# A decoder layer on one core: another order of the first splits and of the attention's steps, heads in alternating halves of the PSUM banks, and the residual rows loaded at two other points

## What is computed

```python
proj = x @ w_in                      # c_b, c_c, c_h, q, k, v, o (1024 wide each), 8 gate columns
y_conv = c_b * causal_dwconv(c_c * c_h, w_sc_conv)
h = mlstm(q, k, v, i_pre, f_pre)     # 4 heads of 256: decay-weighted causal scores, times v, normalised
h = sigmoid(o) * head_layer_norm(h)
x = layer_norm(alpha * x + concat(y_conv, h) @ w_out)
hid = causal_dwconv(x @ w_up) + b;  val, gate = split(hid)
out = layer_norm(alpha * x + (silu(gate) * val) @ w_down)
```

## Time and profile before

| | |
|---|---|
| time, median of 3 runs | 2162.56 us (2161.64 to 2162.69) |
| the profiled execution's own time | 2164.61 us |
| its span, first to last instruction | 2162.8 us |
| PE busy with matmuls | 2081.5 us (96%) |
| DVE / ACT / POOL busy | 1787.0 / 1055.2 / 328.5 us |
| mean granted TensorE clock | 0.986 of full speed |

### The profile page before, as it was taken

One profiled execution on the slowest core, in us unless ns is written; L12 is line 12 of the kernel. 1 busy time (PEld: TensorE's weight loads), 2 busy tenths in 40 slices (PEclk: granted clock), 3 DMA queues, 4 the chain that ended last, 5 costly groups with the idle time before them and its releaser, 6 DMA issues. The chain is left out here.

```text
span 2162.8 us, 28480 instructions
## 1 busy us (share of the span) xinstructions
PE 2081.5 (96%) x10903; PEld 1782.9 (82%) x10903; DVE 1787.0 (83%) x2188; ACT 1055.2 (49%) x1310; POOL 328.5 (15%) x305
## 2 busy tenths in 40 slices
PE   9899999998998998999999999999999999999995
PEld 7788888886876887888888888888888878888874
DVE  7687777776437997988888888888888789999998
ACT  5344444444324446555555555555555455444442
POOL 2011101100001304011111111111011023221220
PEclk9999999999999999999999999999999999999998
DMA  6788877752238625898888887887778888775463
GB/s 221 213 214 207 204 193 189 182 162 101 78 122 258 181 70 158 224 246 235 218 210 211 238 222 198 214 235 211 192 196 218 268 233 224 205 244 145 137 194 78
DMA packets 115815, 419.02 MB, mean 194 GB/s; under 512 B 10988, under 2 KB 25356, under 8 KB 109408
## 3 DMA queue, kind: packets, MB, share of 16 engines
q1 hardware_dynamic: 75648, 270.56, 35.5%
q0 software_dynamic: 40032, 146.64, 35.1%
HBM read 353.72 MB, written 31.46 MB: 178 GB/s over the span
## 5 line engine op out<-in xcount | busy, mean ns | idle before, releaser
L2346 PE MATMUL ps<-xb,slot_hi 128*128 128x512 f32 x2408 | 605.7, 393 | 9.1 <-DVE hid L1831 9.0
L2346 PEld LDWEIGHTS ps<-xb,slot_hi 128*128 128x128 f32 x2408 | 433.9, 189 | 89.1 <-issue 9.5
L2350 PEld LDWEIGHTS ps<-xb,slot_lo 128*128 128x128 f32 x2400 | 328.2, 191 | 23.6
L2350 PE MATMUL ps<-xb,slot_lo 128*128 128x256 f32 x2400 | 335.4, 283 | 0.0
L2210 PE MATMUL ps<-xm,m_slot_hi 128*128 128x512 f32 x1120 | 282.3, 394 | 8.7 <-DVE m_hid L1495 8.7
L2210 PEld LDWEIGHTS ps<-xm,m_slot_hi 128*128 128x128 f32 x1120 | 202.5, 190 | 45.6 <-issue 9.2
L1800 DVE TENSOR_TENSOR slot_lo<-unit_odd,slot_hi 128x1024 fp32r<-128x1024 f32 x153 | 187.1, 1223 | 34.5 <-ACT slot_hi L1168 34.5
L1168 ACT ACTIVATE slot_hi<-unit_odd 128x1024 fp32r<-128x1024 f32 x154 | 162.8, 1058 | 106.9 <-PE ps L2350 75.6
L1800 DVE TENSOR_TENSOR slot_lo<-unit_even,slot_hi 128x1024 fp32r<-128x1024 f32 x147 | 179.7, 1222 | 36.0 <-ACT slot_hi L1168 35.7
L1168 ACT ACTIVATE slot_hi<-unit_even 128x1024 fp32r<-128x1024 f32 x147 | 155.5, 1058 | 94.3 <-PE ps L2350 75.6
L2386 PE MATMUL ps<-slot_hi,hc 128*128 128x512 f32 x744 | 184.8, 390 | 4.7 <-DVE acc L1997 4.7
(11 more groups left out here) (257 smaller groups left out, 3414.1 us busy)
## 6 DMA issues: line engine op xcount, KB each, us to landing
unit_odd<-w_up SPq DMA_DIRECT2D x88, 512.0 KB, 6.2
unit_even<-w_up SPq DMA_DIRECT2D x84, 512.0 KB, 6.5
da<-w_down SPq DMA_DIRECT2D x16, 2048.0 KB, 11.9
unit_odd<-w_up POOLq DMA_DIRECT2D x44, 512.0 KB, 8.5
unit_even<-w_up POOLq DMA_DIRECT2D x42, 512.0 KB, 8.5
m_unit_odd<-w_feat SPq DMA_DIRECT2D x40, 512.0 KB, 4.4
m_unit_even<-w_feat SPq DMA_DIRECT2D x40, 512.0 KB, 4.5
da<-w_down POOLq DMA_DIRECT2D x20, 1024.0 KB, 10.5
```

The costliest lines, as they stand in the source:

```text
L2346: pe.matmul(ps[:, up_bank(m, i), :], hi[:, P * j:P * j + P], xb[:, i, j, :, :].rearrange("p r t -> p (r t)"), start=fresh and j == 0, stop ...
L2350: last = pe.matmul(ps[:, up_bank(m, i), 256:512], lo[:, P * j:P * j + P], xb[:, i, j, 0, :], start=False, stop=j == 7, skip_group_check=no ...
```

## The change

- The first tiles: ACT and DVE split tile 5 straight after tile 4 and put the sums of x between the later splits; the subtraction for P7 goes from POOL to DVE (`sum_raw(3)`). Two `raw` buffers swap places, so that block A21 of the mix weights (which S1 needs) is loaded after the split of tile 6 and A12 after that of tile 7, the other way round than before. ACT splits the second mix product's weights before it copies v out of the banks.
- The gates' arithmetic starts one product later and its first block is cut into four steps, one for each of n = 4..7; all later gate steps come four products later.
- `spread_g(0)` no longer waits for the last mix sums; its bank is 1 in place of 2 (`scores(0)` now has the wait).
- Banks: q8..q15 accumulate in banks 0 to 3; heads 0 and 1 have scores in banks 2 and 3, heads 2 and 3 in 6 and 7; the values of heads 0, 1 and 3 are in banks 0 to 3, those of head 2 in 4 to 7. Which waits this moves is seen in the diff.
- Steps of the heads after other tiles (`SPREAD`, `SCORE`, `VALUE`); on ACT and DVE the reading of the last v and o tiles comes ahead of the other steps of its tile.
- `x_rows` h = 1 is loaded when head 3's norm is done, h = 0 where both were loaded.

```diff
-SPREAD = {STAGE0 - 1: 0, STAGE0 + 3: 1, STAGE0 + 7: 2, STAGE0 + 11: 3}
-SCORE = {STAGE0 + 1: 0, STAGE0 + 4: 1, STAGE0 + 8: 2, STAGE0 + 12: 3}
-VALUE = {STAGE0 + 2: 0, STAGE0 + 6: 1, STAGE0 + 10: 2, STAGE0 + 14: 3}
+SPREAD = {STAGE0 - 1: 0, STAGE0 + 3: 1, STAGE0 + 8: 2, STAGE0 + 12: 3}
+SCORE = {STAGE0 + 1: 0, STAGE0 + 5: 1, STAGE0 + 10: 2, STAGE0 + 14: 3}
+VALUE = {STAGE0 + 2: 0, STAGE0 + 6: 1, STAGE0 + 11: 2, STAGE0 + 16: 3}
+SCORE_BANK, VALUE_BANK = (2, 2, 6, 6), (0, 0, 4, 0)
...
+        def row_bank(r):
+            return 0 if V1_LAST < r <= O_LAST[0] else 4
...
-            for b, r in ((A12, 6), (A21, 7), (A22, 8)):
+            for b, r in ((A21, 6), (A12, 7), (A22, 8)):
...
-            pool.wait_ge(t_raw, 1)
-            pool.tensor_tensor(t_raw_of["P7"], x_quarter(1, 1), x_quarter(0, 1), ALU.subtract).then_inc(t3_raw, 1)
             mix_s1(1)
...
+                if c == 0:
+                    pool.wait_ge(norm_step, 13 * HEADS)
+                    pool.wait_ge(p_l, HEADS)
+                    pool.wait_ge(g_spread, HEADS)
+                    load_rows(1)
                 for p in (0, 2):
                     out_s1(c, p)
                 if c == 0:
                     pool.wait_ge(y_turned, 8)
-                    for h in (1, 0):
-                        pool.dma_start(rows[:, 2 * h:2 * h + 2, :], x_rows[2 * h:2 * h + 2].rearrange("c p n -> p c n")
-                                       ).then_inc(res_in[h], 16)
+                    load_rows(0)
...
             split(4)
+            split(5)
             sum_raw(0)
             sum_raw(1)
-            split(5)
+            split(6)
             sum_raw(2)
             sum_lo(0)
-            split(6)
+            sum_raw(3)
+            split(7)
             sum_lo(1)
             sum_lo(2)
-            split(7)
             sum_lo(3)
...
-                if n == 3:
-                    gates_a()
-                if n == 5:
+                if 4 <= n < 8:
+                    gates_a(n - 4)
+                if n == 9:
                     gates_b()
...
-                        if first and kk == 0 and r == STAGE0 and c < 2:
-                            if c == 0:
+                        if first and kk == 0 and c == 0:
+                            if r == STAGE0:
                                 pe.wait_ge(hid_dve, N_READS * (N_UNITS - 1) + READS["P3"])
-                        elif first and kk == 0 and r == V1_LAST + 1:
-                            pe.wait_ge(vp_lo, NS + c + 1)
-                        elif first and kk == 0 and r == O_LAST[0] + 1:
-                            pe.wait_ge(o_sig, c + 1)
-                        last = mm3(ps[:, B_ROWS + c, :], x_block(k, c, later),
+                            elif r == V1_LAST + 1:
+                                pe.wait_ge(head_read, 2 * NS)
+                            elif r == O_LAST[0] + 1:
+                                pe.wait_ge(head_read, 3 * NS)
+                                pe.wait_ge(p_raw, HEADS * NS)
+                        last = mm3(ps[:, row_bank(r) + c, :], x_block(k, c, later),
...
-                    pe.wait_ge(hid_dve, N_READS * N_UNITS)
                 else:
                     pe.wait_ge(head_read, NS * h)
+                    if h == 2:
+                        pe.wait_ge(vp_lo, 2 * NS)
-                pe.matmul(ps[:, B_S, :], head_rows[:, h, :], g_row[:, :], start=True, stop=True).then_inc(g_spread, 1)
+                pe.matmul(ps[:, SCORE_BANK[h] - 1, :], head_rows[:, h, :], g_row[:, :], start=True, stop=True).then_inc(g_spread, 1)
...
+                if h == HEADS - 1:
+                    pe.wait_ge(o_sig, NS)
```

More of the change, by code:

```diff
@@ L158, in build @@
         eps = at("eps", [P, 2], SM + 3424)
-        raw = [at(f"raw{i}", [P, 1024], WR + a * KB) for i, a in enumerate((28, 32, 20, 24))]
+        raw = [at(f"raw{i}", [P, 1024], WR + a * KB) for i, a in enumerate((28, 32, 24, 20))]
         w_hi = [at(f"w_hi{i}", [P, 1024], WR + (36 + 4 * i) * KB, F32R) for i in range(SPLIT)]
@@ L724, in out_s1, with load_rows @@
                                accum_op=ALU.add, max_dma_last_dim=4096).then_inc(s1_added[p // 2], 16)
+            def load_rows(h):
+                pool.dma_start(rows[:, 2 * h:2 * h + 2, :], x_rows[2 * h:2 * h + 2].rearrange("c p n -> p c n")
+                               ).then_inc(res_in[h], 16)
             def out_s3(c, p):
@@ L902, in sum_split @@
                 what = SUMS[i]
[L903 to L906, removed]
+                act.wait_ge(t_raw, i + 1)
                 act.activation(xm[:, SLOT[what], :, 0, :], t_raw_of[what], ACT.Copy,
@@ L1039, in _ @@
             split(9)
+            mix_split(1)
             act.wait_ge(tile_done, GATES)
             for c in range(NS):
-                act.activation(v_stage[:, c, :], ps[:, B_ROWS + c, :], ACT.Copy).then_inc(v_got, 1)
-            mix_split(1)
+                act.activation(v_stage[:, c, :], ps[:, 4 + c, :], ACT.Copy).then_inc(v_got, 1)
             act.wait_ge(consts_in, 16 * 7)
@@ L1082, in rows_work @@
             def rows_work(r):
+                if r == V1_LAST:
+                    act.wait_ge(tile_done, r + 1)
+                    act.wait_ge(pv_done, 2 * NS)
+                    for c in range(NS):
+                        act.activation(v_hi[:, c, :, 0:HD], ps[:, row_bank(r) + c, :].rearrange("p (h e) -> p h e", h=2),
+                                       ACT.Copy).then_inc(vp_hi, 1)
+                if r in O_LAST:
+                    act.wait_ge(tile_done, r + 1)
+                    if r == O_LAST[0]:
+                        act.wait_ge(scores_done, NS * HEADS)
+                    else:
+                        act.wait_ge(y_ready, NS)
+                    for c in range(NS):
+                        act.activation(sig[:, c, :], ps[:, row_bank(r) + c, :], ACT.Sigmoid).then_inc(o_sig, 1)
                 if r in SPREAD:
@@ L1096, in rows_work @@
                     act.activation(std[:, :], mv[:, :, 1], ACT.Sqrt, bias=eps[:, 0:1]).then_inc(head_std, 1)
[L1097 to L1110, removed]
             split(STAGE0 + 2)
@@ L1628, in rows_work_b @@
             def rows_work_b(r):
+                if r == V1_LAST:
+                    for c in range(NS):
+                        dve.wait_ge(vp_hi, NS + c + 1)
+                        dve.tensor_tensor(v_lo[:, c, :, 0:HD], ps[:, row_bank(r) + c, :].rearrange("p (h e) -> p h e", h=2),
+                                          v_hi[:, c, :, 0:HD].bitcast(F32), ALU.subtract).then_inc(vp_lo, 1)
                 if r in SPREAD:
@@ L1643, in rows_work_b @@
                     norm_heads(VALUE[r])
-                if r == V1_LAST:
-                    for c in range(NS):
-                        dve.wait_ge(vp_hi, NS + c + 1)
-                        dve.tensor_tensor(v_lo[:, c, :, 0:HD], ps[:, B_ROWS + c, :].rearrange("p (h e) -> p h e", h=2),
-                                          v_hi[:, c, :, 0:HD].bitcast(F32), ALU.subtract).then_inc(vp_lo, 1)
                 if r in O_LAST:
@@ L2149, in scores @@
                         at = P * j
-                        last = mm3(ps[:, B_S + j % 2, 0:SC_W[j]],
+                        last = mm3(ps[:, SCORE_BANK[h] + j % 2, 0:SC_W[j]],
                                    (qk_hi[:, 2 + d, at:at + P], qk_lo[:, 2 + d, at:at + P]),
@@ L2226, in _ @@
                 mix_product(n)
[L2227 removed]
+                if n == 33:
                     turn_gates()
```

83 lines of the change are left out of this document (43 added, 40 removed).

## The result

The changed kernel takes 2126.6 us, median of 4 runs (2125.0 to 2134.2); the kernel before, on the same chip, 2162.2 us (4 runs). The ratio is 0.984, 95% interval 0.982 to 0.987: 1.6% faster. The forecast was 2123.0 us in a range of 2118 to 2131. The profiled execution, the fastest of the four, took 2125.04 us with a span of 2123.3, the very numbers that the prediction gives for it.

The account below looks back on a forecast made before the run. The prediction took PE's time as the bound, with 43.5 us of stops and slow stretches in reach; less 2.0, 0.9, 0.8 and 0.3 us this gave 39.5 us, so 2123.0 us, range 2118 to 2131.

Parts of the forecast that it names:

- The base: PE's time within reach: 33.0 us of stops, 1.8 of overlaps and 8.7 of slow stretches, 43.5 in all.
- First tiles: Tiles 5 and 6: w_lo stops of 1.7 us go; POOL's subtraction on DVE, 1.2 to 2.5 us, is covered.
- The 0.82 us at tile 1: PE's wait in front of tile 1, ahead of everything the change moves; expected to stay.
- A21 ahead of A12: Start of mix stage: A21's earlier load moves the S1, S2, S3 chain about 5.4 us earlier, removing P7's 3.1 us stop.
- The gates and the mix turns: Mix stage: gates in four steps remove P3's 5.6 us stop; longer DVE turns cost 0.8 us, bounds 0 to 3.2.
- spread_g(0): Before q0: the 1.1 us stop for bank 2 goes, and with it the slow q0, 1.75 us.
- scores(0): Third score block's wait for a bank that DVE reads: the stop grows to 2.0 us, bounds 0.7 to 3.7.
- half slow tile: Lower clock after the stop in scores(0): between 0 and 1.75 us, half taken, 0.9.
- Margins: spread_g(2) and values(3): v_lo's margin near half a us, values(3) just covered; each miss 0 to 2 us, taken as 0.
- Rows of x: Residual sums: the 8.4 us stop for load h = 1 goes; h = 0 may be late, 0 to 5.2 us, taken as 0.3.
- the rival of 2130 us: Residual rows: load h = 0 becomes the stop, up to 5.2 us, and the slow part of 2.1 stays; chance 0.14.
- The clock rival: Tiles q1 to q23 held at the lower clock: slower than before, 2177 us with ten such tiles; chance 0.02.

Follow-up runs that it names:

- e2_heads: The kernel before with only the heads' part: step tables, banks of heads, v and o tiles, and their waits; 2145.6 us, ratio 0.992.
- e3_rows: The kernel before with only the residual rows' loads at their new places; 2155.9 us, ratio 0.996.
- e10_pool_sum: The changed kernel with P7's sum of x back on POOL, the splits staying ahead of the sums; 2127.4 us, ratio 0.983.
- e8_a12_first: The changed kernel with A12 loaded ahead of A21 again and the two raw buffers in their old order; 2127.4 us, ratio 0.984.
- e12_again: The changed kernel measured once more with no edit; 2129.7 us, ratio 0.985.
- e5_s2_load: The changed kernel with A21 going out first, ahead of A11, among the second unit's weight loads; 2124.1 us, ratio 0.982.
- e11_old_banks: The changed kernel with v and o tiles back in banks 4 to 7 and heads in 0 to 3, steps at their new tiles; 2136.8 us, ratio 0.987.
- e1_first: The kernel before with only the first part: splits ahead of sums, P7's sum on DVE, A21 first, gates in steps; 2154.0 us, ratio 0.996.

## Why the prediction was right

**The base held.** That stops are worth their idle time plus 0.16 us plus their slow stretch is borne out where nothing else mixes in: from spread_g(1) to the transposes of y the prediction has 16.4 us and 16.4 were won, in the whole change and in e2_heads; the residual rows have 10.4, and 10.4 were won, in the whole change and in e3_rows alone.

**First tiles.** Both w_lo stops are gone: 2.0 forecast, 1.9 measured. P7's sum takes 2.28 us on DVE, within the 1.2 to 2.5 given, and its cover held (e10_pool_sum: no matter where it is done). The 0.82 us at tile 1, which the prediction let stand, are not in this profile; they come and go with the execution (0.79 in e8_a12_first, none in e12_again), so the sum has luck in it here as well.

**A21 ahead of A12.** The effect was right (P7's 3.1 us gone), but the cause given isn't needed: e8_a12_first has A12 first and no stop at P7. The new splits had moved the whole chain.

**The gates and the mix turns** are the step that failed. The prediction put 0.8 us (0 to 3.2) on the excess of DVE's turns, as work. It came to 4.0 us, outside the bounds. The work is as forecast, 0.8 us (e5_s2_load). The rest the prediction did not have: 1.5 us of wait, S2's for a DMA of the next unit, with PE's next sums queued behind it, and 1.6 us of the lower clock after the stop. That unit's loads go out when the mix stage starts (58.80 us, 60.73 before), so they don't get earlier with what PE gains inside the stage. The prediction asked what stood behind a wait for each wait that the change adds; this one was in the code before, at no cost because PE was late.

**spread_g(0)** and the slow q0: gone as forecast, 11.6 - 8.6 = 3.0 us by q1.

**scores(0)**: forecast 2.0 and 0.9 for its clock. The stop is 1.25 us, inside the bounds, and the clock cost nothing: from it to spread_g(1) PE takes 16.1 us in all nine profiles that have it, and the granted clock is 1.00 (468.8 to 486.5 us after the change). The Trainium skill's section that the prediction set against its half slow tile ("TensorE: Matmul & The Clock Gate", "HAM oscillation — how this bites in real kernels") was right here. P4 differs from it: a stop of 2.19 us there was followed by a stretch at the lower clock that cost 1.6 us, and the measurement decides.

**Margins.** v_lo was the narrow one: DVE's four splits end at 519.68 + 2.48 = 522.16 and spread_g(2) starts at 522.71, 0.55 us later, near the half us forecast. But "the reading comes first in DVE's queue" is no edit with an effect: with the new tables no step shares the tiles at which v and o are read. And the prediction gave all 7.4 us ahead of q8 to the banks; e11_old_banks gives them 3.2, and the rest to the steps' new tiles.

**Rows of x.** POOL's issues after, and their landing:

```profile
590.54 0.71 POOL L728 DMA_DIRECT2D stream<-x_rows  x1 [50.34 <-DVE stream L1457]
...
634.31 0.74 POOL L728 DMA_DIRECT2D stream<-x_rows  x1 [18.23 <-PE ps L2202]
```
```profile
L728 POOL DMA_DIRECT2D stream<-x_rows x2: 706/723/740, 590.5 to 634.3; - x2
...
DMA to landing us min/median/max: 8.0/12.8/17.5
```

Load h = 1 takes 8.0 us and lands at 598.5, 44.6 us before its first use at 643.1. Load h = 0 takes 17.5, near the 18.1 assumed, and lands at 651.8, 1.5 us ahead of its first use at 653.3: the rival of 2130 us was 1.5 us away from making DVE wait; how much more PE would have borne was not measured.

**What evened out.** P4 cost 3.2 us more than forecast, scores(0) 1.5 less, and 1.6 us came, by luck, from the layer norm, where the stretch from its first transposes to the first up product takes 40.0 us after and 41.6 before, and between 40.0 and 41.6 in all fourteen profiles. The clock rival (slower than before) was wrong: the stretch 520 to 590 us, with hardly a stop in it, has a granted clock of 1.00, and the mean of the whole is 0.992, 0.986 before. Window of the changed kernel (us, then busy us and instructions of PE, PEld, DVE, ACT, POOL; PE clock, DMA share, GB/s):

```profile
520.00:590.00 70.00, 70.00 (x344) 57.93 (x343) 43.39 (x93) 28.56 (x34) 0.75 (x1) 1.00 0.29 91
```

## What to carry over

When a change brings PE earlier, go through the waits that cost nothing before: one that hangs on a DMA issued ahead of the place where PE gains keeps its time, and whatever stands behind it in that engine's queue can become the next stop. A stop has two parts, the queue's order and the buffer; try the order alone first, since here it was worth 4.2 of 7.4 us. And add up gains place by place in the profile: the end of the span scatters by some us from one late DMA, and hits by luck.

## What the hardware showed that was not expected

The clock after a stop is not told by the stop's length. At products of the mix stage, where eight matmuls take 2.00 us at full clock, a stop of 2.65 us was followed by 2.08 in one profile (e8_a12_first) and by 3.52 in another (e2_heads), one of 2.01 by 3.10 (e1_first), one of 3.05 by 2.08 (the kernel before, P7). The granted clock goes down or not after stops of 2 to 4 us; a price for it is a range, not a value.

A split of DVE that starts while POOL's 128x2048 subtraction runs ends only after it: in e10_pool_sum POOL is done at 29.75 + 6.73 = 36.48 and DVE's split at 37.56; in the kernel before the same split took 2.64 us, from 33.12 to 35.76, with POOL done at 34.68. Both end 1.08 us after POOL (1.09 in e2_heads and e3_rows), near a split's own 1.22, as though it had run only then. POOL's 6.72 us fit a wait of the same kind, though no run has the subtraction by itself: in the kernel before a sum of DVE's had begun 0.05 us ahead of it and ends at 27.91 + 2.29 = 30.20, and from there POOL takes 4.48 us (4.49 in e10_pool_sum). The Trainium skill ("SBUF — State Buffer", "Who interferes with whom") has the port pair that the two share as an exclusive lock, and the numbers agree.
